# PEER gates: both buffers on their way to memory kept through the early down stage, their stores awaited at the first reload; one more modulation row in the search

## The chip, the cores and the metric

The kernel runs on one core of one Trainium2 chip. The metric is the device time of one execution in microseconds (us). In the text the engines are TensorE (PE, with PEld for its weight loads), VectorE (DVE), ScalarE (ACT), GpSimd (POOL) and SyncE (SP). VectorE, ScalarE and TensorE each work through their own instructions in order; they meet at semaphores.

## What is computed

The program computes three transformer blocks on 256 tokens of width 1024, one after the other. The change lies in the PEER feed-forward layer of the first block, which picks 16 of 128 x 128 experts for each of 8 heads and each token:

```python
q = (xt @ w_q).reshape(n_tok, PEER_HEADS, 2, PEER_KEY_HALF)
s = jnp.einsum('thpk,pnk->thpn', q, sub_keys)
top_s, top_i = lax.top_k(s, PEER_TOPK)
...
best_s, best_pos = lax.top_k(cand_s, PEER_TOPK)
experts = jnp.take_along_axis(cand_i, best_pos, axis=-1)
gates = jax.nn.softmax(best_s, axis=-1)
...
hid = gelu(einsum('chkd,cd->chk', u_tab[ec], xc))
y = einsum('chk,chkd->cd', gc * hid, v_tab[ec])
```

and in the modulation vectors of the third block, `mod = silu(c) @ ada_w[layer] + ada_b[layer]`, which need nothing but inputs and so are computed early, in 24 rows of 512 columns, wherever an engine has room.

## The kernel before, in words

The kernel does not gather experts. It computes the hidden value of every expert column group for all tokens and multiplies it by a dense table of gates that is zero where an expert was not picked. The 128 x 128 experts are worked as 128 groups ("keys" in the code, experts below) of 128. The first 40 (`EARLY`) have their hidden values (`early_up`, then GELU into `acted` or `late`) computed ahead, beside the search and the spread of the gates.

Weights come through one ring of four chunks of 2 MB (`ring`), filled by SyncE in the order of one stream. A chunk is asked for when the chunk four places ahead of it is released, which happens at the first matmul of the chunk behind that one, so SyncE is three chunks ahead of TensorE. The stream's order in these stages is written out by hand: `SEARCH_CHUNKS` for the search and `SPREAD_CHUNKS` for the spread of the gates, where `u` is a chunk with the up weights of four early experts and `a` one modulation row (`ada_row`, 8 matmuls into bank 4, L1430).

Four stages matter here.

1. **The search** (L1569 on). VectorE finds the top 16 in two halves of tokens. TensorE meanwhile works through `SEARCH_CHUNKS`, and ScalarE takes each early expert through GELU (L1638). ScalarE works in order: 14 early experts, the exponential of the first half's scores (`found`, L1640), 14 more, the exponential of the second half. VectorE needs that exponential for the sum of gates (L1626). At the end TensorE transposes `found` (L1664) and ScalarE copies it to `expert`.
2. **The spread** (`spread_gates`, L1725). In 32 batches of eight tokens VectorE makes one-hot rows and columns, TensorE multiplies them into the dense gates (L1837), in 64 steps of four tokens, and ScalarE copies them out of PSUM: 16 of the 128 experts stay in `gates` (L1808), the other 112 go to one of two buffers, `away_first` and `away_last` (L1812), by turns of 16 tokens, and from there to `kept_gates` in memory (L1815). Behind the matmuls of every second step TensorE has a piece of `SPREAD_CHUNKS`: half an early expert or one modulation row. At its end ScalarE copies the ten rows summed so far into `mod` (L1820) and waits until the stores of `away_first` have landed (L1821), since that buffer lives in this stage only. TensorE ends with 18 warm-up matmuls (`keep_warm`, L558, products of ones that nobody reads).
3. **The early down stage** (`early_down`, L1865). For each of the 40 early experts VectorE scales its hidden values by the gates into `full` (L1918); ScalarE rounds `full` and the down weights to `hidden_hi` and `down_hi` (L1903, L1891), VectorE makes the remainders `down_lo` and `hidden_lo` (L1924, L1926), and TensorE adds three products to banks 4 to 7 (L1943, L1949, L1953). ScalarE splits the weights of the first expert and then waits for the stores of both buffers (L1899, L1900) ahead of the loop. Behind every eighth expert it reloads eight experts' gates from `kept_gates` (`load`, L1893), for use from expert 16 on.
4. **The feed-forward loop** (`feed_forward`, L1123) does the other 88 experts, with the rest of the rows on VectorE.

A stage is a block: all engines meet at its end before the next one starts.

Of the kernel before, what the change touches and what calls it, by code (L numbers as in the profile page):

```python
# [20 lines left out]
BF16 = mybir.dt.bfloat16  # L21
# [5 lines left out]
P = 128  # L27
TOKENS = 256
# [22 lines left out]
SPAN = 16  # L51
GROUP = 8
EARLY = 40
SEARCH_CHUNKS = "uuauuuauu"
SPREAD_CHUNKS = "auaauaauaaa"
FORWARD_CHUNKS = "ff" + 14 * "afff"
ROWS_ON_PE = (SEARCH_CHUNKS + SPREAD_CHUNKS).count("a")
LATE_ROWS = [n for n, kind in enumerate(FORWARD_CHUNKS) if kind == "a"]
# [336 lines left out]
def build(nc, d, widths, offsets):  # L395
    ctx = ExitStack()
    with ctx:
        names = {}

        def buffer(name, shape, dt=F32):  # L400

            names[name] = names.get(name, 0) + 1
            return nc.sbuf_tensor(name if names[name] == 1 else f"{name}_{names[name]}", shape, dt)

        def sbuf(name, shape, dt=F32, mem=ctx):
            return mem.enter_context(buffer(name, shape, dt))
# [1009 lines left out]
        def peer(mem):  # L1416
# [251 lines left out]
            with ExitStack() as dense:  # L1668
                gates = sbuf("gates", [P, KEPT // GROUP, TOKENS // SPAN, GROUP, SPAN], mem=dense)
                work = hT[:, 0:4, :].rearrange("p (a b) n -> p a b n", a=2)  # L1670
                with ExitStack() as early:
                    away_last = sbuf("away_last", [P, KEYS - KEPT, SPAN], mem=early)
                    late = sbuf("acted_late", [P, EARLY - n_early, TOKENS], mem=early)
                    acted_of = lambda e: acted[:, e, :] if e < n_early else late[:, e - n_early, :]
                    spread_gates(expert, key_no, gates, away_last, acted_of, ada_row, early_up)
                    early_down(acted_of, gates, work)
                buf_2, p = params("ln2", dense)
                row_sums = sbuf("row_sums", [P, 4, WIDE], mem=dense)
                feed_forward("peer", KEYS - EARLY, ACT.Gelu, x_parts, scale_by=gates, starts=False, work=work, ahead=(buf_2[:], d["ln2"]),
                             rows=(lambda k: cond_at[:, k, BAND - 1:BAND], one_at, row_sums))  # L1680
# [41 lines left out]
            act.dma_start(gates[:, slot].rearrange("p b j m -> p b (j m)"),  # L1722
                          src.rearrange("b p n -> p b n")).then_inc(gates_loaded[slot], 16)

        def spread_gates(expert, key_no, gates, away_last, acted_of, ada_row, early_up):  # L1725

# [16 lines left out]
            with signals("dve_step", "parts_ready", "columns_ready", "weighed", "placed", "placed_read", "early_ready", "early_read",  # L1745
# [3 lines left out]
                    buffer("number", [P, 2, TOKENS], BF16) as number, buffer("keys", [P, KEYS, near], BF16) as keys, \  # L1749
                    buffer("row_hot", [P, 2, batch // near, KEYS, near], BF16) as row_hot, \  # L1750
                    buffer("col_hot", [P, 2, batch // near, KEYS, near], BF16) as col_hot, \
                    buffer("col_gate", [P, 2, 3, batch // near, KEYS, near], BF16) as col_gate, \
                    buffer("away_first", [P, KEYS - KEPT, SPAN]) as away_first, nc.Block() as block:
                away = (away_first, away_last)
                gate_rest = away_last[:].rearrange("p j m -> p (j m)")[:, 0:2 * TOKENS].rearrange("p (a n) -> p a n", a=2)

                @block.sync
                def _(sp):
# [34 lines left out]
                @block.scalar  # L1793
                def _(act):
                    early = [n for n, (kind, _, half) in enumerate(extra) if kind == "u" and half % 2]

                    def keep_early(n):

                        if n in early:
                            e = early.index(n)  # L1800
                            act.wait_ge(early_ready, e + 1)
                            act.activation(acted_of(first_early + e), ps[:, 5 + e % 3, 0:TOKENS], ACT.Gelu).then_inc(early_read, 1)

                    for s in range(steps):
                        n, at = s // per_block, s % per_block * few
                        got = ps[:, s % 4, :].rearrange("p (m j) -> p j m", m=few)
                        act.wait_ge(placed, s + 1)
                        act.activation(gates[:, :, n, :, at:at + few], got[:, 0:KEPT, :].rearrange("p (g j) m -> p g j m", j=GROUP),  # L1808
                                       ACT.Copy)
                        if n >= 2 and at == 0:  # L1810
                            act.wait_ge(gates_stored[n % 2], 16 * (n // 2))
                        act.activation(away[n % 2][:, :, at:at + few], got[:, KEPT:KEYS, :], ACT.Copy).then_inc(placed_read, 1)  # L1812
                        if s % per_block == per_block - 1:
                            act.wait_ge(placed_read, s + 1)
                            act.dma_start(kept_gates[n], away[n % 2][:].rearrange("p j m -> p (j m)")).then_inc(gates_stored[n % 2], 16)  # L1815
                        if s % 2 and s >= 3:
                            keep_early(s // 2 - 1)
                    keep_early(batches - 1)
                    act.wait_ge(mod_ready, 1)
                    act.activation(mod[:], ps[:, 4, :], ACT.Copy)  # L1820
                    act.wait_ge(gates_stored[0], 16 * (blocks // 2))  # L1821

                @block.tensor
                def _(pe):
                    e = 0
                    row = first_row
                    keep_warm(pe, 23, 5)
                    for s in range(steps):
                        b = s // 2 % 2
                        if s % 2 == 0:  # L1830
                            pe.wait_ge(weighed, s // 2 + 1)
                        if s >= 4:
                            pe.wait_ge(placed_read, s - 3)
                        for m in range(few):
                            g, o = (s % 2 * few + m) // near, m % near
                            for a in range(3):
                                last = pe.matmul(ps[:, s % 4, m * KEYS:m * KEYS + KEYS], row_hot[:, b, g, :, o],  # L1837
                                                 col_gate[:, b, a, g, :, o], start=(a == 0), stop=(a == 2))
                        last.then_inc(placed, 1)
                        if s % 2 == 0 or s // 2 >= len(extra):  # L1840
                            continue
                        kind, _, half = extra[s // 2]
                        if half == 0:
                            w = stream.slot(stream.take(pe))
                        if kind == "a":
                            last = ada_row(pe, w, row)
                            row += 1
                            if row == ROWS_ON_PE:
                                last.then_inc(mod_ready, 1)
                        else:  # L1850
                            if half % 2 == 0 and e >= 3:
                                pe.wait_ge(early_read, e - 2)
                            last = early_up(pe, w, half // 2, range(4 * (half % 2), 4 * (half % 2) + 4), 5 + e % 3)
                            if half % 2:
                                last.then_inc(early_ready, 1)
                                e += 1
                        if half == 0:
                            stream.pending = True
                    pe.wait_ge(early_read, EARLY - first_early)
                    keep_warm(pe, 18, 5)  # L1860

        def early_down(acted_of, gates, work):

# [6 lines left out]
            with signals("full_ready", "high_ready", "hidden_ready", "down_done", "down_hi_ready", "down_split") as (  # L1870
# [12 lines left out]
                @block.scalar  # L1883
                def _(act):
                    def split_down(j):

                        if j % 4 == 0:
                            stream.wait(act, first + j // 4)
                        if j >= 2:
                            act.wait_ge(down_done, j - 1)  # L1890
                        act.activation(down_hi[:, j % 2, :], raw(j), ACT.Copy).then_inc(down_hi_ready, 1)  # L1891

                    def load(group):  # L1893

                        act.wait_ge(full_ready, GROUP * (group + 1))
                        load_gates(act, gates, group % (KEPT // GROUP), group)

                    split_down(0)
                    for n, stored in enumerate(gates_stored):  # L1899
                        act.wait_ge(stored, 16 * (TOKENS // SPAN // 2))  # L1900
                    for j in range(EARLY):
                        act.wait_ge(full_ready, j + 1)
                        act.activation(hidden_hi[:, j % 2, :], full[:, j % 2, :], ACT.Copy).then_inc(high_ready, 1)  # L1903
                        if j % GROUP == GROUP - 1:
                            load(j // GROUP)
                        if j + 1 < EARLY:
                            split_down(j + 1)
# [22 lines left out]

                @block.tensor
                def _(pe):
                    keep_warm(pe, 10, 0)
                    for j in range(EARLY):
                        hi, lo = down_hi[:, j % 2, :], down_lo[:, j % 2, :]
                        pe.wait_ge(down_split, j + 1)
# [1890 lines left out]
```

## Time and profile before

| | |
|---|---|
| median of 3 runs | 3170.78 us (3165.64 to 3172.79) |
| profiled execution | 3165.71 us |
| its span in the trace | 3164.0 us |
| its mean granted TensorE clock | 0.981 of full |
| TensorE busy | 3001.0 us (95%) |
| VectorE busy | 2312.5 us (73%) |
| ScalarE busy | 1570.1 us (50%) |
| DMA mean | 206 GB/s |

Times in the trace are us from the start of the span. The search lies at 375 to 485, the spread at 485 to 598, the early down stage at 598 to 725. A row of the timeline has the start, the time that the group of instructions took, the engine (PEld, ACTq and SPq are TensorE's weight loads and the queues that issue DMAs), the line in the kernel, the output and inputs, and the count. In square brackets stands how long the engine was idle before it, and what released it. A DMA issue's own time is that of issuing; how long the transfer took to land is in the DMA views.

### The profile page before, as it was taken

What the parts mean: (1) busy time and instruction counts of PE and PEld (TensorE: products, weight loads), DVE (VectorE), ACT (ScalarE), POOL (GpSimd) and SP (SyncE); (2) the same over time, 40 slices, a digit from 0 to 9 for tenths busy, and PEclk for the clock granted to TensorE, in tenths of its full rate; (3) what the DMA queues carried; (4) which work ended last, traced back from release to release, by engine and by line L of the source; (5) the groups of instructions that cost most, each with busy time, mean ns of one, the idle gap of its engine ahead of it and who ended that gap; (6) DMA issues with size and microseconds to landing.
All of it is one profiled execution on the core that took longest, in us unless ns stands there. A gap on an engine that the chain in (4) does not pass through costs nothing. (4 is left out here: it accounts for less than half of the span.)

```text
span 3164.0 us, 45210 instructions
## 1 busy us (share of the span) xinstructions
PE 3001.0 (95%) x17980; PEld 2532.8 (80%) x17980; DVE 2312.5 (73%) x3604; ACT 1570.1 (50%) x2500; POOL 96.5 (3%) x135
## 2 busy tenths in 40 slices
PE   8999999999999999979999899989998889999997
PEld 7897887678888887757877688768886679999997
DVE  6466599668888886387765677757656768888887
ACT  4443313444444444264443544644345368878875
POOL 0000000000000001200000000000001000000000
PEclk9999999999999999899998999999999889999999
DMA  7344456866777764314542254424542068989895
GB/s 297 146 180 166 150 199 238 317 216 253 283 262 273 285 253 182 134 54 149 190 156 104 107 186 160 160 80 160 184 181 100 1 246 325 341 332 332 324 340 196
DMA packets 81262, 652.05 MB, mean 206 GB/s; under 512 B 6168, under 2 KB 35352, under 8 KB 38704
## 3 DMA queue, kind: packets, MB, share of 16 engines
q1 hardware_dynamic: 49872, 620.05, 52.5%
q10 hardware_dynamic: 31200, 29.36, 2.9%
q8 instruction: 132, 2.16, 0.3%
q14 instruction: 58, 0.48, 0.0%
HBM read 633.66 MB, written 15.73 MB: 205 GB/s over the span
## 5 line engine op out<-in xcount | busy, mean ns | idle before, releaser
L1238 PE MATMUL ps<-x_both,up_hi 128*128 128x512 f32 x1568 | 559.2, 396 | 2.4 <-DVE up_lo L1338 2.1
L369 DVE TENSOR_TENSOR weight_lo<-ring,weight_hi 128x1024 fp32r<-128x1024 f32 x236 | 289.5, 1238 | 231.6 <-ACT weight_hi L362 231.0
L1242 PE MATMUL ps<-x_both,up_lo 128*128 128x256 f32 x1568 | 440.7, 281 | 0.0
L1238 PEld LDWEIGHTS ps<-x_both,up_hi 128*128 128x128 f32 x1568 | 294.4, 188 | 76.6 <-DVE up_lo L1338 3.4
L362 ACT ACTIVATE weight_hi<-ring 128x1024 fp32r<-128x1024 f32 x236 | 245.6, 1053 | 162.4 <-PE ps L542 95.2
L1242 PEld LDWEIGHTS ps<-x_both,up_lo 128*128 128x128 f32 x1568 | 295.8, 189 | 6.3
L3529 DVE TENSOR_TENSOR up_lo<-ring,up_hi 128x1024 fp32r<-128x1024 f32 x242 | 294.3, 1217 | 5.1 <-ACT up_hi L3648 5.1
L520 PE MATMUL ps<-x_both,weight_hi 128*128 128x256 f32 x1024 | 291.2, 284 | 3.4 <-DVE weight_lo L369 2.5
L521 PE MATMUL ps<-x_both,weight_hi 128*128 128x256 f32 x1024 | 288.6, 282 | 0.0
L522 PE MATMUL ps<-x_both,weight_lo 128*128 128x256 f32 x1024 | 288.4, 282 | 0.0
L3446 PE MATMUL ps<-up_hi,taken_hi 128*128 128x256 f32 x968 | 285.6, 295 | 2.1 <-DVE seat L3533 2.1
L1256 PE MATMUL ps<-down_hi,hidden_hi 128*128 128x512 f32 x696 | 274.2, 394 | 1.3 <-DVE hidden_lo L1370 1.3
L3448 PE MATMUL ps<-up_hi,taken_lo 128*128 128x256 f32 x968 | 274.2, 283 | 0.0
L3447 PE MATMUL ps<-up_lo,taken_hi 128*128 128x256 f32 x968 | 274.2, 283 | 0.0
L1260 PE MATMUL ps<-down_lo,hidden_hi 128*128 128x512 f32 x696 | 272.9, 392 | 0.0
L3648 ACT ACTIVATE up_hi<-ring 128x1024 fp32r<-128x1024 f32 x242 | 256.0, 1059 | 25.4 <-PE ps L3448 24.9
L1338 DVE TENSOR_TENSOR up_lo<-ring,up_hi 128x1024 fp32r<-128x1024 f32 (+1 forms) x174 | 235.5, 1354 | 17.2 <-ACT up_hi L1299 17.2
L1343 DVE TENSOR_TENSOR down_lo<-ring,down_hi 128x1024 fp32r<-128x1024 f32 x174 | 212.4, 1221 | 24.4 <-ACT down_hi L1305 23.7
L1305 ACT ACTIVATE down_hi<-ring 128x1024 fp32r<-128x1024 f32 x174 | 183.7, 1056 | 64.2 <-PE ps L1264 64.1
L1264 PE MATMUL ps<-down_hi,hidden_lo 128*128 128x512 f32 x696 | 214.4, 389 | 0.0
L1299 ACT ACTIVATE up_hi<-ring 128x1024 fp32r<-128x1024 f32 (+1 forms) x174 | 201.0, 1156 | 5.6 <-PEq L1874 4.8
L520 PEld LDWEIGHTS ps<-x_both,weight_hi 128*128 128x128 f32 x1024 | 195.2, 191 | 7.2 <-DVE weight_lo L369 3.8
(552 smaller groups left out, 6318.9 us busy)
## 6 DMA issues: line engine op xcount, KB each, us to landing
ring<-in_stream SPq DMA_DIRECT2D x180, 2048.0 KB, 7.7
ring<-in_experts SPq DMA_DIRECT2D x121, 1536.0 KB, 8.6
ring<-in_stream SPq DMA_DIRECT2D x22, 1536.0 KB, 6.3
gates<-kept_gates ACTq DMA_DIRECT2D x14, 1024.0 KB, 9.0
kept_gates<-away_first ACTq DMA_DIRECT2D x8, 896.0 KB, 5.2
kept_gates<-away_last ACTq DMA_DIRECT2D x8, 896.0 KB, 7.7
params_mix<-in_mix SPq DMA_DIRECT2D x1, 3072.0 KB, 22.7
ring<-in_stream SPq DMA_DIRECT2D x4, 512.0 KB, 7.6
```

The source lines that it names most:

```text
L369: dve.tensor_tensor(self.place(self.lo, b), self.raw(b), self.place(self.hi, b), ALU.subtract).then_inc(self.split, 1)
L520: first = pe.matmul(out, hi[:, k, :], x_parts[0][:, k, :], start=(k == 0), stop=False)
L521: second = pe.matmul(out, hi[:, k, :], x_parts[1][:, k, :], start=False, stop=False)
L522: last = pe.matmul(out, lo[:, k, :], x_parts[0][:, k, :], start=False, stop=(k == DK - 1))
L1238: last = pe.matmul(out, hi[:, o:o + P], x_both[:, k, :, :].rearrange("p a n -> p (a n)"), start=(k == 0), stop=(k == DK - 1), skip_group_c ...
L1242: last = pe.matmul(out[:, 0:TOKENS], lo[:, o:o + P], x_hi[:, k, :], start=False, stop=(k == DK - 1), skip_group_check=True)
L1256: last = pe.matmul(out, hidden_hi[:, j % 2, tokens], hi[:, o:o + WIDE], start=(starts and i is None and j == 0), stop=False, skip_group_ch ...
L1260: pe.matmul(out, hidden_hi[:, j % 2, tokens], lo[:, o:o + WIDE], start=False, stop=False, skip_group_check=True)
L3446: pe.matmul(to, taken_hi[:, s % 3, k, :], hi, start=(k == 0), stop=False, skip_group_check=True)
L3447: pe.matmul(to, taken_hi[:, s % 3, k, :], lo, start=False, stop=False, skip_group_check=True)
L3448: last = pe.matmul(to, taken_lo[:, s % 3, k, :], hi, start=False, stop=(k == DK - 1), skip_group_check=True)
L3529: dve.tensor_tensor(up_part(up_lo, g, half), raw_up(g, half), up_part(up_hi, g, half), ALU.subtract).then_inc(up_split, 1)
```

## The change

The edit does four things. It allocates both `away` buffers outside of the spread stage, so that they live until the early down stage is over. It takes the wait for `gates_stored[0]` out of the end of the spread, and moves the waits for both stores from ahead of the early down loop into `load`, ahead of the first reload of gates (group 0, behind expert 7). It moves one modulation row from the end of `SPREAD_CHUNKS` (11 chunks before, 10 after) to `SEARCH_CHUNKS` (9 before, 10 after): the second row of the search now comes behind 16 early experts and a third behind 24, where the second stood behind 20. And it cuts the warm-up matmuls from 18 to 9 at the end of the spread and from 10 to 7 at the start of the early down stage. The number of rows that TensorE does (ten) and of early experts (28 and 12) stays.

```diff
--- before.py
+++ after.py
@@ -51,8 +51,8 @@
 SPAN = 16
 GROUP = 8
 EARLY = 40
-SEARCH_CHUNKS = "uuauuuauu"
-SPREAD_CHUNKS = "auaauaauaaa"
+SEARCH_CHUNKS = "uuauuauuau"
+SPREAD_CHUNKS = "auaauaauaa"
 FORWARD_CHUNKS = "ff" + 14 * "afff"
 ROWS_ON_PE = (SEARCH_CHUNKS + SPREAD_CHUNKS).count("a")
 LATE_ROWS = [n for n, kind in enumerate(FORWARD_CHUNKS) if kind == "a"]
@@ -1669,10 +1669,10 @@
                 gates = sbuf("gates", [P, KEPT // GROUP, TOKENS // SPAN, GROUP, SPAN], mem=dense)
                 work = hT[:, 0:4, :].rearrange("p (a b) n -> p a b n", a=2)
                 with ExitStack() as early:
-                    away_last = sbuf("away_last", [P, KEYS - KEPT, SPAN], mem=early)
+                    away = [sbuf(n, [P, KEYS - KEPT, SPAN], mem=early) for n in ("away_first", "away_last")]
                     late = sbuf("acted_late", [P, EARLY - n_early, TOKENS], mem=early)
                     acted_of = lambda e: acted[:, e, :] if e < n_early else late[:, e - n_early, :]
-                    spread_gates(expert, key_no, gates, away_last, acted_of, ada_row, early_up)
+                    spread_gates(expert, key_no, gates, away, acted_of, ada_row, early_up)
                     early_down(acted_of, gates, work)
                 buf_2, p = params("ln2", dense)
                 row_sums = sbuf("row_sums", [P, 4, WIDE], mem=dense)
@@ -1722,7 +1722,7 @@
             act.dma_start(gates[:, slot].rearrange("p b j m -> p b (j m)"),
                           src.rearrange("b p n -> p b n")).then_inc(gates_loaded[slot], 16)
 
-        def spread_gates(expert, key_no, gates, away_last, acted_of, ada_row, early_up):
+        def spread_gates(expert, key_no, gates, away, acted_of, ada_row, early_up):
 
 
 
@@ -1749,10 +1749,8 @@
                     buffer("number", [P, 2, TOKENS], BF16) as number, buffer("keys", [P, KEYS, near], BF16) as keys, \
                     buffer("row_hot", [P, 2, batch // near, KEYS, near], BF16) as row_hot, \
                     buffer("col_hot", [P, 2, batch // near, KEYS, near], BF16) as col_hot, \
-                    buffer("col_gate", [P, 2, 3, batch // near, KEYS, near], BF16) as col_gate, \
-                    buffer("away_first", [P, KEYS - KEPT, SPAN]) as away_first, nc.Block() as block:
-                away = (away_first, away_last)
-                gate_rest = away_last[:].rearrange("p j m -> p (j m)")[:, 0:2 * TOKENS].rearrange("p (a n) -> p a n", a=2)
+                    buffer("col_gate", [P, 2, 3, batch // near, KEYS, near], BF16) as col_gate, nc.Block() as block:
+                gate_rest = away[1][:].rearrange("p j m -> p (j m)")[:, 0:2 * TOKENS].rearrange("p (a n) -> p a n", a=2)
 
                 @block.sync
                 def _(sp):
@@ -1818,7 +1816,6 @@
                     keep_early(batches - 1)
                     act.wait_ge(mod_ready, 1)
                     act.activation(mod[:], ps[:, 4, :], ACT.Copy)
-                    act.wait_ge(gates_stored[0], 16 * (blocks // 2))
 
                 @block.tensor
                 def _(pe):
@@ -1857,7 +1854,7 @@
                         if half == 0:
                             stream.pending = True
                     pe.wait_ge(early_read, EARLY - first_early)
-                    keep_warm(pe, 18, 5)
+                    keep_warm(pe, 9, 5)
 
         def early_down(acted_of, gates, work):
 
@@ -1893,11 +1890,12 @@
                     def load(group):
 
                         act.wait_ge(full_ready, GROUP * (group + 1))
+                        if group == 0:
+                            for stored in gates_stored:
+                                act.wait_ge(stored, 16 * (TOKENS // SPAN // 2))
                         load_gates(act, gates, group % (KEPT // GROUP), group)
 
                     split_down(0)
-                    for n, stored in enumerate(gates_stored):
-                        act.wait_ge(stored, 16 * (TOKENS // SPAN // 2))
                     for j in range(EARLY):
                         act.wait_ge(full_ready, j + 1)
                         act.activation(hidden_hi[:, j % 2, :], full[:, j % 2, :], ACT.Copy).then_inc(high_ready, 1)
@@ -1930,7 +1928,7 @@
 
                 @block.tensor
                 def _(pe):
-                    keep_warm(pe, 10, 0)
+                    keep_warm(pe, 7, 0)
                     for j in range(EARLY):
                         hi, lo = down_hi[:, j % 2, :], down_lo[:, j % 2, :]
                         pe.wait_ge(down_split, j + 1)
```

## Rows read from the trace of the kernel before

**Rows 1.** The page's busy times: us, share of the span, instructions.
```profile
PE 3001.0 (95%) x17980; PEld 2532.8 (80%) x17980; DVE 2312.5 (73%) x3604; ACT 1570.1 (50%) x2500; POOL 96.5 (3%) x135
```

**Rows 2.** Timeline from 586 to 612: start, us, engine, line, operation.
```profile
586.80 6.99 SPq L314 DMA_DIRECT2D ring<-in_stream  x3
...
592.39 1.92 PE L1430 MATMUL ps<-ring,cond_at 128*32 128x512 f32 x16
...
593.18 0.33 ACTq L1815 DMA_DIRECT2D kept_gates<-away_last  x1
...
594.24 4.06 PE L562 MATMUL ps<-ones 128*128 128x512 bf16 x18
594.38 0.60 ACT L1820 ACTIVATE mod<-ps 128x512 f32<-128x512 f32 x1 [1.23 <-PE ps L1430]
...
598.58 1.06 ACT L1891 ACTIVATE down_hi<-ring 128x1024 fp32r<-128x1024 f32 x1 [3.60 <-PEq L1753]
598.60 2.32 PE L562 MATMUL ps<-ones 128*128 128x512 bf16 x10 [0.30 <-PEq L1753]
...
599.67 1.23 DVE L1924 TENSOR_TENSOR down_lo<-ring,down_hi 128x1024 fp32r<-128x1024 f32 x1 [0.64 <-ACT down_hi L1891]
604.87 0.42 ACT L1903 ACTIVATE hidden_hi<-hT 128x256 fp32r<-128x256 f32 x1 [5.23 <-DMA kept_gates<-away_last]
...
605.31 0.43 DVE L1926 TENSOR_TENSOR hidden_lo<-hT,hidden_hi 128x256 fp32r<-128x256 f32 x1 [4.42 <-ACT hidden_hi L1903]
...
605.89 0.77 PE L1943 MATMUL ps<-down_hi,hidden_hi 128*128 128x512 f32 x1 [4.97 <-DVE hidden_lo L1926]
...
611.14 0.40 PE L1943 MATMUL ps<-down_hi,hidden_hi 128*128 128x512 f32 x1
```

**Rows 3.** Windows: stretch, us, busy of PE to POOL, clock, DMA share, GB/s.
```profile
606.00:611.00 5.00, 5.00 (x12) 3.94 (x13) 1.97 (x4) 0.53 (x2) 0.00 (x0) 0.50 0.94 341
```

**Rows 4.** DMA issues from 584 to 607: count, KB each, median us to landing.
```profile
ring<-in_stream SPq DMA_DIRECT2D x4, 2048.0 KB, 12.2
kept_gates<-away_first ACTq DMA_DIRECT2D x1, 896.0 KB, 4.5
kept_gates<-away_last ACTq DMA_DIRECT2D x1, 896.0 KB, 11.6
```

**Rows 5.** Timeline of ScalarE around the second row of the search (at 447.82).
```profile
447.92 0.38 ACT L1638 ACTIVATE acted<-ps 128x256 f32<-128x256 f32 x1 [3.07 <-PE ps L1439]
453.43 0.38 ACT L1638 ACTIVATE acted<-ps 128x256 f32<-128x256 f32 x1 [5.12 <-PE ps L1439]
```

**Rows 6.** Timeline of the end of the search.
```profile
477.60 0.38 ACT L1638 ACTIVATE acted<-ps 128x256 f32<-128x256 f32 x1 [3.07 <-PE ps L1439]
...
479.30 0.31 ACT L1640 ACTIVATE found<-found 128x128 f32<-128x128 f32 x1
479.74 2.29 DVE L1624 TENSOR_REDUCE found<-sums 128x128 f32<-128x2048 f32 x1
```

**Rows 7.** Timeline of TensorE after two other pauses.
```profile
725.61 1.89 PE L562 MATMUL ps<-ones 128*128 128x512 bf16 x8 [0.32 <-PEq L1874]
...
2450.87 12.33 PE L3256 MATMUL ps<-q_dec,k_dec 128*128 128x64 f32 x64 [4.77 <-DVE k_dec L3036]
```

**Rows 8.** Timeline of TensorE from the search into the spread, and VectorE's first batch.
```profile
477.40 0.49 PE L1664 MATMUL ps<-ident,found 128*128 128x128 f32 x3
...
482.96 0.90 PE L1664 MATMUL ps<-ident,found 128*128 128x128 f32 x3 [5.07 <-DVE found L1628]
...
485.13 6.67 PE L562 MATMUL ps<-ones 128*128 128x512 bf16 x23 [1.26 <-PEq L1570]
...
488.77 1.89 DVE L1790 TENSOR_TENSOR col_gate<-col_hot,gate_part 128x1024 bf16<-128x1024 bf16 x3
...
491.63 1.54 PE L1837 MATMUL ps<-col_gate,row_hot 128*128 128x128 bf16 x24
```

**Rows 9.** Windows: the same columns as in rows 3, in the spread.
```profile
520.00:560.00 40.00, 40.00 (x439) 31.32 (x438) 38.77 (x63) 17.30 (x55) 0.00 (x0) 1.00 0.81 318
```

## The prediction, made before the change was run

> **What bounds the kernel now.** I read the page's busy times first. TensorE is busy for 3001 of the 3164 us of the span and VectorE for 2312 [rows 1], so nearly everywhere a change is worth what it takes off TensorE's way, and elsewhere only what it takes off a pause of TensorE. The change touches the end of the spread stage (`spread_gates`) and the start of the stage after it (`early_down`), so I read the order of time there [rows 2]. TensorE places the last tokens, runs one modulation row for 1.92 us from 592.39, then 18 warm-up matmuls for 4.06 us from 594.24 to 598.30. The block ends, and `early_down` begins on ScalarE at 598.58. TensorE gives ten more warm-ups and then sits idle for 4.97 us, until 605.89. The reader should follow the releasers back: TensorE waits for `hidden_lo`, that for `hidden_hi` on ScalarE, and `hidden_hi` at 604.87 is released by the store of `away_last`, 5.23 us after ScalarE had been ready. That wait is lines 1899 and 1900, which stand ahead of the loop. Third, the granted clock [rows 3]: from 606 to 611 it is 0.50, the lower level, 1.2 GHz, after TensorE's pause. The first expert of the loop therefore takes from 605.89 to 611.14, 5.25 us. Fourth, the transfers [rows 4]: the store of `away_last`, issued at 593.18 [rows 2], needed 11.6 us, because three ring loads of 2 MB were issued within 586.80 to 593.79 and share the DMA with it; the last store of `away_first` needed 4.5 us and had landed at about 591.0. For the search stage I read how far TensorE's work is from the end of VectorE's [rows 5, 6].
>
> **Part 1: the shorter end of the spread stage.** The row moved out ran behind the last placed tokens, with nothing of TensorE's beside it: 594.24 - 592.39 = 1.85 us of TensorE's path. Warm-ups go from 18 to 9: 18 took 4.06 us, a lone one about 0.38, so one more costs (4.06 - 0.38) / 17 = 0.2165 us and nine take 8 x 0.2165 + 0.38 = 2.11. That removes 1.95 us. TensorE now ends at 592.39 + 2.11 = 594.50 instead of 598.30: **3.8 us** earlier. What is late next? ScalarE's last copy out of PSUM and its DMA issue end at 593.51 (593.18 and 0.33 of issue), and the copy of `mod` (0.60 us [rows 2]) needs no later row any more: it ends near 594.1, 0.4 us ahead of TensorE. SyncE has one ring load fewer to issue there. The wait for `gates_stored[0]` that is taken out costs nothing now (that store had landed at about 591.0), so its removal is worth 0. A block's end does not itself wait for transfers: the store of `away_last` was under way across the end at 598.3 [rows 2, 4].
>
> **Part 2: the store wait moved to the first reload.** From the block's end at 598.30, ScalarE splits the first weights at 598.58 (1.06), VectorE follows at 599.67 (1.23) and ends at 600.90 [rows 2]. `hidden_hi` then no longer waits for anything but its turn: it would run from 599.67 to 600.09 beside VectorE's work. `hidden_lo` takes 0.43 and TensorE begins 0.15 behind it, as at 605.89. So TensorE's first real matmul stands 600.90 + 0.40 + 0.15 = 601.45, that is 3.15 us behind the block's end instead of 7.59: **4.44 us** gone. Seven warm-ups instead of ten cost 0.65 us less and end before 596.4; they are hidden under this chain either way, worth 0. New start of the first expert: 594.50 + 3.15 = 597.65 against 605.89, 8.24 us in all. The wait itself comes back at expert 7, where it stands on ScalarE ahead of one DMA issue and of `split_down(8)`, for which VectorE and TensorE would wait. It is reached after seven experts of some 2.7 us, at about 617, and the store had landed by 604.9 even with one more load in the way. Its cost is that of two waits already satisfied; no row isolates one, so between 0 and 0.1 us, and I take 0, since 12 us of margin cover it.
>
> **Part 3: the clock.** The first expert took 5.25 us at 1.2 GHz [rows 2, 3], which is 2.6 us at 2.4 GHz. TensorE's pauses there become 0.3 us at the block's end and 597.65 - 594.8 - 1.7 = 1.15 us behind the seven warm-ups. The nearest row is the next change of stage, at 725.61, where a pause of 0.32 us was followed by eight warm-ups in 1.89 us, at the full rate [rows 7]. So I take the clock as kept: **2.6 us** gained; the ends are 0 and 2.6.
>
> **Part 4: one more row in the search.** TensorE works there without a pause until 477.9 [rows 8]. A row costs it the distance between two results with a row between, less the usual one: (453.43 - 447.92) - (3.07 + 0.38) = 5.51 - 3.45 = 2.06 us [rows 5]. The new row stands behind the 16th expert, so the first half's exponential (behind the 14th) does not move. The second half's does: it ends now at 479.61 and would end at 481.67; VectorE, busy with its own reduction, asks for it at 482.03 [rows 6]. The row fits, with 0.36 us to spare: cost **0**, and if that cover were short at most 2.06. Its chunk is asked for three chunks ahead, over 20 us of TensorE's work, against 12.2 us for a load in the busiest stretch [rows 4]. Each later load keeps its moment in the spread stage and only moves up in what it carries, so that the last of the three loads of 586.80 to 593.79 disappears. The first chunk of `early_down` is asked for a whole group of experts earlier; the second at 586.80 and needed after four experts, near 608.
>
> TensorE's pause at 477.9 to 482.96 shrinks from 5.07 to 3.0 us. It is followed now by transposes of 0.90 us instead of 0.49 and by 23 warm-ups that take 6.67 us instead of 5.15 at the full rate, so that the first placement starts at 491.63 where its operands stood ready at 490.7 [rows 8]. The spread stage behind it leaves TensorE no gap (40.00 of 40 us busy, VectorE 38.77 [rows 9]), so a start earlier by up to 0.4 + 0.9 = 1.3 us would go through to the end. Whether 3 us keep the clock I can't tell: 4.77 us of pause at 2450.87 was followed by a long slow group, 12.33 us for 64 matmuls [rows 7]. Between a gain of 1.3 and a loss of 2 (the clock falling later, under the warm-ups) I take 0, as the pause was not shown to be short enough. The Trainium skill, "TensorE: Matmul & The Clock Gate", Part 1, says that the observation is free-running and does not start with the kernel's work, so equal pauses can end differently. By that sentence the sum would hold either end here; no run shown here tests it.
>
> **The sum.** 3.8 + 4.44 + 2.6 + 0 = 10.84 us off. What lies behind is ordered by TensorE's own progress and moves as a whole. The profiled execution took 3165.71 us (span 3164.0 and 1.7 around it), so it would be 3154.9. It stands 5.1 us below the median of the three runs shown, 3170.78; the median becomes **3159.9 us**, 0.34% less. The three runs lie 7.2 us apart, and about 0.2% (6.3 us) is what a measurement of this kernel can tell from no change.
>
> **The rivals.**
> A. The clock falls in spite of the warm-ups, because they are fewer: the first expert stays at 5.25 us. For it: a pause of TensorE came ahead of each slow stretch in these rows. Against it: the shortest pauses [rows 7]. The 2.6 us are lost: 3162.5.
> B. The added row isn't covered: the 0.36 us of margin are short, VectorE waits for its exponential and the whole rest slips by up to 2.06 us: 3162.0.
> C. The stall is moved, not removed: the store isn't down at expert 7, or the reload behind it is late for expert 16. `hidden` data of expert 8 then wait as they do now and most of the 4.44 us and the 2.6 us come back: 3167. Against it: 12 us of margin, and 2 MB less in the way.
> D. The edit doesn't do what it says, that is, some other wait holds the block's end or `hidden_hi`: then only the row and the warm-ups count, 3.8 us minus a longer pause behind them, 3167 to 3171. Against it: the profile names the store as the releaser.
> E. Slower: pauses all shift against the clock's changes. A slow stretch as at 2450.87 costs about 5 us (12 us at half the rate). From the third such new stretch on the gain is used up; with four and more, 20 - 10.8 = 9 us over: 3180. For it: slow stretches do follow pauses, and the search's and the spread's pauses change. Against it: the pauses here get shorter, and other stages keep theirs.
>
> **How the numbers follow.** Forecast 0.62; A 0.13; B 0.08; C 0.06; D 0.07; E 0.04. Forecast, A and B give 0.83, but the last two lie only 2 us inside the 6.3 us bound and the runs scatter by several us, so faster 0.80, within 0.2% 0.16, slower 0.04. The range reaches from 3159.9 less the 1.3 us of part 4 and half of the scatter (3.6 us), 3155, with a little more for a row or copy that I counted too high, 3153, up to rivals A and B with the same scatter, 3166.5.
>
> **What would show it.** TensorE's last warm-up of the spread stage ends near 594.5, `hidden_hi` of the first expert starts behind `down_hi` with no DMA named, TensorE's pause ahead of the first expert is near 1.2 us instead of 4.97, the granted clock there is 1.00 and the second expert starts near 600.3 instead of 611.14. In the search, `found` is exponentiated until 481.7 and VectorE names no wait for it in the second half. The prediction is wrong if `gate_sum` waits for `found` there, if a releaser `kept_gates` appears at expert 7, or if the clock is at 0.50 behind 597.

## The result and the profile after

The changed kernel takes 3158.78 us (median of 7 runs, 3156.89 to 3159.56), the kernel before 3169.24 us (7 runs, 3165.64 to 3172.79): 10.5 us less, ratio 0.9967 with a 95% interval of 0.9957 to 0.9977. The two profiled executions are 3165.71 and 3158.78 us, only 6.9 apart: the profiled execution of before lies at the fast end of its runs, whose lowest is 3165.64.

The place of the change, as the profile after has it, is this. The timeline's columns are as in [rows 2]; the last line of the first fence is the second expert of the loop.

```profile
586.19 3.67 SPq L314 DMA_DIRECT2D ring<-in_stream  x2
...
590.30 1.55 PE L1834 MATMUL ps<-col_gate,row_hot 128*128 128x128 bf16 x24
...
591.69 2.10 PE L562 MATMUL ps<-ones 128*128 128x512 bf16 x9
...
592.58 0.33 ACTq L1813 DMA_DIRECT2D kept_gates<-away_last  x1
592.95 0.60 ACT L1818 ACTIVATE mod<-ps 128x512 f32<-128x512 f32 x1 [0.40 <-ACT away_last L1810]
594.07 1.06 ACT L1888 ACTIVATE down_hi<-ring 128x1024 fp32r<-128x1024 f32 x1 [0.52 <-PEq L1752]
...
594.09 1.67 PE L562 MATMUL ps<-ones 128*128 128x512 bf16 x7 [0.30 <-PEq L1752]
595.03 0.40 ACT L1901 ACTIVATE hidden_hi<-hT 128x256 fp32r<-128x256 f32 x1
...
596.87 0.47 PE L1941 MATMUL ps<-down_hi,hidden_hi 128*128 128x512 f32 x1 [1.10 <-DVE hidden_lo L1924]
...
599.67 0.39 PE L1941 MATMUL ps<-down_hi,hidden_hi 128*128 128x512 f32 x1
```

Against [rows 2], `hidden_hi` no longer names a store, TensorE's pause ahead of the first expert is 1.10 us instead of 4.97, and that expert lasts from 596.87 to 599.67, 2.80 us instead of 5.25. The window below shows the clock, third from the end: 1.00 where [rows 3] had 0.50.

```profile
597.00:602.00 5.00, 5.00 (x23) 4.13 (x24) 2.90 (x5) 1.79 (x3) 0.00 (x0) 1.00 1.01 423
```

The moved wait stands where the first reload of gates is issued. The timeline there shows ScalarE going on without a pause of its own:

```profile
614.35 1.06 ACT L1888 ACTIVATE down_hi<-ring 128x1024 fp32r<-128x1024 f32 x1 [1.36 <-PE ps L1951]
614.74 0.39 ACTq L1722 DMA_DIRECT2D gates<-kept_gates  x1
615.32 0.40 ACT L1901 ACTIVATE hidden_hi<-hT 128x256 fp32r<-128x256 f32 x1
```

The store, issued at 592.58, took 11.6 us here too and landed at 604.2, 10.5 us ahead of that reload:

```profile
kept_gates<-away_last ACTq DMA_DIRECT2D x1, 896.0 KB, 11.6
```

And the end of the search, which now has one row more:

```profile
479.26 0.49 PE L1664 MATMUL ps<-ident,found 128*128 128x128 f32 x3
482.75 0.55 PE L1664 MATMUL ps<-ident,found 128*128 128x128 f32 x3 [3.00 <-DVE found L1628]
484.57 6.81 PE L562 MATMUL ps<-ones 128*128 128x512 bf16 x23 [1.27 <-PEq L1570]
491.21 1.54 PE L1834 MATMUL ps<-col_gate,row_hot 128*128 128x128 bf16 x24
...
481.16 0.31 ACT L1640 ACTIVATE found<-found 128x128 f32<-128x128 f32 x1
...
481.85 0.29 DVE L1626 TENSOR_REDUCE gate_sum<-found 128x8 f32<-128x128 f32 x1
```

`gate_sum` follows VectorE's own reduction with no wait named, as in [rows 6]; the exponential ends 0.35 us ahead of the time at which it is asked for.

To compare the two profiles without what happened earlier, I count from the first placement (491.63 in [rows 8], 491.21 here) to the second expert (611.14 in [rows 2], 599.67 here): 119.51 and 108.46 us, 11.05 less. At the first matmul of the feed-forward loop the changed kernel is 11.1 us ahead in time from the span's start (727.96 against 716.84).

### The profile page after: what moved, and what is told of

Its sections match the earlier page's. It is cut to its first block and busy times, and to the rows that moved or that the text cites. A ratio compares the mean times of both kernels' runs of the same rounds, so it can differ in the third digit from the quotient of the medians.

```text
span 3157.0 us, 45185 instructions
## 1 busy us (share of the span) xinstructions
PE 3003.0 (95%) x17968; PEld 2533.3 (80%) x17968; DVE 2313.1 (73%) x3604; ACT 1569.8 (50%) x2500; POOL 96.7 (3%) x135
```

## The experiments

All are timed against the kernel before, in two groups of four. The kernel before took 3167.96 us beside the first four and 3169.58 beside the last four.

**The wait alone.** Buffers and waits as in the change, rows and warm-ups as before. The cut is against the changed kernel:

```diff
-SEARCH_CHUNKS = "uuauuauuau"
-SPREAD_CHUNKS = "auaauaauaa"
+SEARCH_CHUNKS = "uuauuuauu"
+SPREAD_CHUNKS = "auaauaauaaa"
...
-                    keep_warm(pe, 9, 5)
+                    keep_warm(pe, 18, 5)
...
-                    keep_warm(pe, 7, 0)
+                    keep_warm(pe, 10, 0)
```

> The kernel before with both buffers living on and the store waits moved to the first reload; the row stays at the end of the spread and the warm-ups stay 18 and 10. Theory 1 (the parts add as in the prediction: a chain of 3.15 us behind the block's end, then the store wait, then the clock): the block ends as before near 598.3, the first expert starts near 601.5 instead of 605.9 and runs at the full clock, so 4.4 + 2.6 = 7.0 us faster. Rival (the store was late only because of the third ring load, and whoever removes that load gets the same): no different here, 7.0, but then row_only shows the same gain. Rival (the clock falls all the same): 4.4.

Measured: 3162.06 us against 3167.96, 5.9 us less, ratio 0.9985 (0.9976 to 0.9994). Timeline of that run:

```profile
597.23 2.32 PE L562 MATMUL ps<-ones 128*128 128x512 bf16 x10 [0.30 <-PEq L1752]
...
600.00 0.47 PE L1941 MATMUL ps<-down_hi,hidden_hi 128*128 128x512 f32 x1 [0.46 <-DVE hidden_lo L1924]
...
602.84 0.39 PE L1941 MATMUL ps<-down_hi,hidden_hi 128*128 128x512 f32 x1
```

The block ends at 596.93 and the first expert starts 3.07 us behind it, as in the changed kernel, where it was 7.59 in the kernel before. The second expert starts at 602.84, so the first takes 2.84 us, and the falling clock, the rival, is not there. Theory 1 holds in the trace: from the first placement (490.25) to the second expert it is 112.59 us against 119.51 in the kernel before, 6.92 less, where 7.0 were expected. The median shows 5.9; its interval allows 1.9 to 7.6 us.

**The row alone.** The kernel before with only this:

```diff
-SEARCH_CHUNKS = "uuauuuauu"
-SPREAD_CHUNKS = "auaauaauaaa"
+SEARCH_CHUNKS = "uuauuauuau"
+SPREAD_CHUNKS = "auaauaauaa"
```

> The kernel before with only the row moved from the spread to the search. Theory 1 (the store sets the first expert whatever TensorE does ahead of it): the store of away_last still lands near 604, as in the changed kernel, where it took 11.6 us too, so 0 to 1 us faster. Rival (the third ring load is what made the store late): it lands near 599 to 600, the pause of TensorE falls under 1.5 us and the clock is kept, 7 to 8 us faster.

Measured: 3167.91 us against 3167.96, ratio 1.0003 (0.9994 to 1.0012): no difference that the times can tell. Its timeline:

```profile
592.26 4.05 PE L562 MATMUL ps<-ones 128*128 128x512 bf16 x18
...
604.34 0.42 ACT L1903 ACTIVATE hidden_hi<-hT 128x256 fp32r<-128x256 f32 x1 [6.70 <-DMA kept_gates<-away_last]
...
605.36 0.76 PE L1943 MATMUL ps<-down_hi,hidden_hi 128*128 128x512 f32 x1 [6.44 <-DVE hidden_lo L1926]
```

And its DMA view for the store (count, KB, us to landing):

```profile
kept_gates<-away_last ACTq DMA_DIRECT2D x1, 896.0 KB, 11.1
```

The block ends 2.0 us sooner (596.31) and TensorE waits 1.5 us longer. The store is issued at 593.15 and takes 11.1 us, 0.5 less than before, although one 2 MB load is missing. That load had been issued at 593.45, 0.3 us behind the store. What the store shares the DMA with here are the two loads issued from 586.76 to 590.43: from 586 to 604 the DMA moves 6.05 MB, which is those two loads and the last two stores. The windows of this run show it at work until the store lands and no longer (the last two columns are the DMA's busy share and GB/s):

```profile
597.00:602.00 5.00, 1.92 (x9) 0.68 (x7) 1.25 (x2) 0.64 (x1) 0.00 (x0) 0.91 0.99 413
602.00:603.00 1.00, 0.00 (x0) 0.00 (x0) 0.00 (x0) 0.00 (x0) 0.00 (x0) 0.50 0.76 314
603.00:604.00 1.00, 0.00 (x0) 0.00 (x0) 0.00 (x0) 0.00 (x0) 0.00 (x0) 0.50 0.09 36
```

So the rival, that the third load made the store late, has fallen.

**The warm-ups alone.** The kernel before with 9 and 7 warm-ups in place of 18 and 10.

> The kernel before with only the warm-ups cut to 9 and 7. Theory 1: they stand ahead of the store wait, which still ends near 604.9; TensorE's pause grows from 5.0 to some 7.6 us, nothing gained: 0 (within 1 us), and the clock is at 0.50 for the first expert. Rival (warm-ups are on the path by themselves): 1.95 us faster.

Measured: 3167.43 us against 3167.96, ratio 0.9999 (0.9990 to 1.0008). The timeline shows the same wait for the store ahead of `hidden_hi` (6.46 us) and something else:

```profile
597.08 1.06 ACT L1891 ACTIVATE down_hi<-ring 128x1024 fp32r<-128x1024 f32 x1 [2.53 <-DMA ring<-in_stream]
...
605.62 0.77 PE L1943 MATMUL ps<-down_hi,hidden_hi 128*128 128x512 f32 x1 [7.71 <-DVE hidden_lo L1926]
```

The block ends at 595.94 now and ScalarE could begin at 596.2, but the first chunk of down weights has not landed before 597.1. With the row still in the spread, that chunk would have been the next wait, 0.9 us long, if the store's were gone. Moving the row asks for the chunk one group of experts sooner, and the wait is absent in the changed kernel.

**All but the moved wait.** The changed kernel with the store waits back ahead of the loop:

```diff
-                        if group == 0:
-                            for stored in gates_stored:
-                                act.wait_ge(stored, 16 * (TOKENS // SPAN // 2))
...
                     split_down(0)
+                    for n, stored in enumerate(gates_stored):
+                        act.wait_ge(stored, 16 * (TOKENS // SPAN // 2))
```

> The changed kernel with one part undone: the waits for both stores stand ahead of the early down loop again (the buffers live on). Theory 1: TensorE is ready at 596.9 but the first expert waits for the store until about 604, and the clock falls: 10 us slower than the changed kernel, 0 to 1 us faster than before. Rival (the ring load made the store late): the store lands near 599 to 600, 3 us slower than the changed kernel at the kept clock, 7 to 8 us faster than before.

Measured: 3168.63 us against 3167.96, ratio 1.0004 (0.9995 to 1.0013). `hidden_hi` waits 8.40 us for the store, TensorE 8.79, and the first matmuls are at the low rate:

```profile
603.68 0.42 ACT L1900 ACTIVATE hidden_hi<-hT 128x256 fp32r<-128x256 f32 x1 [8.40 <-DMA kept_gates<-away_last]
...
604.71 0.77 PE L1940 MATMUL ps<-down_hi,hidden_hi 128*128 128x512 f32 x1 [8.79 <-DVE hidden_lo L1923]
```

Counted from the first placement (491.33), the block ends 4.1 us sooner than in the kernel before, but the first expert starts only 0.9 sooner (113.38 us instead of 114.26), 0.7 of it because the store took 10.9 us here instead of 11.6. The rest is waited away. Gains by the medians: the wait alone 5.9 us, the row alone 0, the warm-ups alone 0.5 and row with warm-ups -0.7 (both inside their intervals around nothing); all together 10.5. The trace agrees for the wait (6.92 us) and for all together (11.05). The row and the warm-ups are worth their 4 us only once the store is out of the way.

**The changed kernel again,** as the measure for the next three, which ran beside it.

> The changed kernel as it is, a second time, as the measure for the other three of this call. Theory 1: about 0.33% under before again, the first expert near 597 at the full clock; what differs between two profiles of it is where the slow clock stretches of later stages fall, a few us of the span. Rival (the measured gain was partly chance): under 0.2%.

Measured: 3158.02 us against 3169.58, ratio 0.9960 (0.9947 to 0.9974). First expert from 596.53 at the full rate, first matmul of the feed-forward loop at 716.25, as in its first profile but for 0.6 us.

**No warm-ups** at the end of the spread and the start of the early down stage (both `keep_warm` lines taken out of the changed kernel).

> The changed kernel without any warm-ups at the end of the spread and the start of the early down stage. Theory 1 (they are there for the clock only): the block ends 0.2 us sooner, set by ScalarE's copy of mod; TensorE pauses for some 4.9 us ahead of the first expert, the clock falls to 0.50 and that expert takes 5.2 instead of 2.8 us: 2.4 us slower than the changed kernel. Rival (a pause of 4.9 us doesn't always cost the clock): 0.2 us faster, first expert at the full clock.

Measured: 3159.28 us against 3158.02 for the changed kernel, ratios to before 0.9966 (0.9954 to 0.9978) and 0.9960 (0.9947 to 0.9974), so the times alone don't tell the two apart. The trace does, first the timeline, then the window of the clock (third from the end):

```profile
597.26 0.77 PE L1939 MATMUL ps<-down_hi,hidden_hi 128*128 128x512 f32 x1 [4.76 <-DVE hidden_lo L1923]
...
602.45 0.40 PE L1939 MATMUL ps<-down_hi,hidden_hi 128*128 128x512 f32 x1
```

```profile
597.00:602.00 5.00, 4.74 (x13) 3.76 (x14) 2.25 (x5) 0.42 (x1) 0.00 (x0) 0.57 0.96 400
```

The pause of 4.76 us brings the clock down and the first expert takes 5.19 us instead of 2.80. Counted from the first placement (491.80, against 490.87 beside it) the first matmul of the feed-forward loop comes 226.96 - 225.38 = 1.6 us later, against 2.4 expected: 2.4 lost on the first expert, 0.2 gained on the block's end, 0.6 recovered in the experts behind. So the warm-ups pay by the clock, as far as this one pair of profiles shows.

**Two rows moved.** The changed kernel with one row more in the search:

```diff
-SEARCH_CHUNKS = "uuauuauuau"
-SPREAD_CHUNKS = "auaauaauaa"
+SEARCH_CHUNKS = "uuauuauuaau"
+SPREAD_CHUNKS = "auaauaaua"
```

> The changed kernel with one more row moved from the spread (its batch 30) to the search, ahead of the last four early experts. Theory 1 (0.35 us of cover is left in the search, each row costs 2.06 there): VectorE's gate_sum waits 1.7 us for found in the second half, the spread starts 1.7 us later and its end comes 1.6 to 1.8 us sooner for the missing row, as TensorE runs behind VectorE there: 0 in sum, within 0.5 us. Rival (the search has more cover than the row of the profile shows): no wait, 1.7 us faster. Rival (spread is set by VectorE, so the row there was free): 1.7 us slower.

Measured: 3157.80 us against 3158.02, ratio to before 0.9965 (0.9951 to 0.9978). The cover in the search is used up, and the wait that the prediction named as its sign is there:

```profile
482.22 0.28 DVE L1626 TENSOR_REDUCE gate_sum<-found 128x8 f32<-128x128 f32 x1 [1.46 <-ACT found L1640]
...
492.52 1.54 PE L1834 MATMUL ps<-col_gate,row_hot 128*128 128x128 bf16 x24
```

The first placement is 1.65 us later than in the changed kernel beside it (492.52 against 490.87). But this profile had begun the search 0.71 us sooner (TensorE's first matmul of the search at 375.24 against 375.95), and the distance stays 0.71 up to the added row. So the second row costs 2.36 us in the search: the wait of 1.46, and 0.93 at the lower clock behind it (the second transposes take 0.90 us instead of 0.55, the 23 warm-ups 7.39 instead of 6.81), less 0.03 elsewhere. From the first placement to the block's end it is 100.84 us (593.36) against 102.58 (593.45), 1.74 less. In sum the second row loses 0.6 us in the trace, a little over the 0.5 that Theory 1 allowed; the medians, 0.2 us apart, don't show it. The rival with more cover and the rival with a free row in the spread both fall. This run also has only one 2 MB load issued ahead of the store, at 587.69, and the store lands sooner:

```profile
kept_gates<-away_last ACTq DMA_DIRECT2D x1, 896.0 KB, 8.7
```

**The exponentials sooner.** The changed kernel with another order on ScalarE in the search:

```diff
-                        for t in range(TT):
-                            for e in range(t * n_early // TT, (t + 1) * n_early // TT):
-                                act.wait_ge(early_ready, e + 1)
-                                act.activation(acted[:, e, :], ps[:, 5 + e % 3, 0:TOKENS], ACT.Gelu).then_inc(early_read, 1)
-                            act.wait_ge(top_ready, t + 1)
-                            act.activation(found[:, t, 2, :], found[:, t, 2, :], ACT.Exp).then_inc(exped, 1)
+                        for e in range(n_early):
+                            act.wait_ge(early_ready, e + 1)
+                            act.activation(acted[:, e, :], ps[:, 5 + e % 3, 0:TOKENS], ACT.Gelu).then_inc(early_read, 1)
+                            if e + 1 in (12, 25):
+                                t = (12, 25).index(e + 1)
+                                act.wait_ge(top_ready, t + 1)
+                                act.activation(found[:, t, 2, :], found[:, t, 2, :], ACT.Exp).then_inc(exped, 1)
```

> The changed kernel with ScalarE's two exponentials of the search moved ahead: the first behind 12 early experts instead of 14, the second behind 25 instead of 28. Theory 1 (VectorE's 4.1 us wait for the first exponential is ScalarE's order and nothing else, and TensorE's early experts end 3.6 us ahead of VectorE): that wait goes, VectorE ends the search near 478.6, the transposes follow TensorE's last early expert without a pause, the block ends 3.0 us sooner, the clock stays at 1.00 and the 23 warm-ups behind take 5.2 instead of 6.8 us, so the first placement starts about 4.0 us sooner: 4.0 us faster than the changed kernel. Rival (the search is set by TensorE's early work alone): 0.4 us.

Measured: 3153.12 us (3152.00 to 3157.32) against 3158.02 for the changed kernel, ratio to before 0.9950 (0.9937 to 0.9964). That is 4.9 us between the medians, though the two intervals overlap. The timeline has the mechanism whole:

```profile
477.78 0.49 PE L1665 MATMUL ps<-ident,found 128*128 128x128 f32 x3
...
478.90 0.55 PE L1665 MATMUL ps<-ident,found 128*128 128x128 f32 x3 [0.63 <-DVE found L1628]
...
480.71 5.12 PE L562 MATMUL ps<-ones 128*128 128x512 bf16 x23 [1.27 <-PEq L1570]
486.31 1.55 PE L1835 MATMUL ps<-col_gate,row_hot 128*128 128x128 bf16 x24 [0.47 <-DVE col_gate L1789]
```

TensorE pauses 0.63 us instead of 3.02 between the transposes, the clock is kept, the 23 warm-ups take 5.12 instead of 6.81 us, and the first placement is at 486.31 instead of 490.87; at the feed-forward loop the lead is 716.25 - 711.71 = 4.5 us. Of this, 1.1 us is not the edit's: this profile began the search at 374.83, the one beside it at 375.95. What remains is 3.4 us, 2.4 for the wait and 1.0 for the clock behind it. VectorE names no wait for `found` any more. In the first half that wait was 4.1 us in the profiles before and after, but 2.4 in the changed kernel's second profile, where TensorE did its first eight early experts in 27.89 us instead of 29.58, at the full clock from the start. The 4.0 us expected were worked out for the wait of 4.1; in this pair it is 3.4, and the medians say 4.9. By its median this is the fastest of the kernels here.

## Why the prediction was right, and where its terms were off

- **The end of the spread** was forecast 3.8 us shorter. From the first placement to the block's end it is 106.67 us before (598.30 - 491.63) and 102.58 after (593.79 - 491.21): 4.09. Of the 0.3 us more, 0.2 lie in the spread itself and 0.1 in the join: the warm-ups begin 591.69 - 590.30 = 1.39 us behind the start of the last placement group, where 1.48 was assumed.
- **The store wait** was forecast at 4.44 us: block's end to first expert is 3.08 us instead of 7.59, 4.51. The run with the wait alone has 3.07, and the one with all but the moved wait shows no gain in its time.
- **The clock** was forecast at 2.6 us: 5.25 - 2.80 = 2.45. The run without warm-ups shows it lost with them gone (rival A in a harder form).
- **The row in the search** was forecast at 0 with 0.36 us to spare; 0.35 was left. The run with a second row shows that a row behind this cover costs 1.46 us of wait and 0.9 us of clock, so the margin was real and rival B had been near.
- **The first pause** was left between a gain of 1.3 and a loss of 2 us, and 0 was taken; that it came out near 0 is luck, as the forecast said it could not tell. The pause shrank to 3.00 us as worked out; the transposes took 0.55 instead of 0.90 us, but the clock fell behind them, and the 23 warm-ups took 6.81 instead of 6.67. In sum about 0.2 us gained. The run with the exponentials sooner shows the gain that was open here: its pause is 0.63 us and its warm-ups take 5.12.
- **The sum** of 10.84 us stands against 11.05 in the trace from the first placement to the second expert, and 10.5 between the medians. From there to the feed-forward loop 0.35 us go back (117.17 us instead of 116.82); no row says where.
- **Rival C** (the stall is moved) had 12 us of margin; it was 10.5. **Rival D** fell with the run of the wait alone. **Rival E** did not come in the medians. It shows between single profiles: from the feed-forward loop's first matmul to the end it is 2436.0 us before, 2440.2 and 2440.5 in the two profiles of the changed kernel, and 2435.7 to 2443.1 over the ten profiles of this study, whose code behind that point is the same. Counted in windows of 2 us, the lower clock takes 98 to 126 us of that rest, and more of it goes with a longer rest (105 us before, 122 after; correlation 0.83), but that this is the cause is only argued. Because of this spread the two profiled spans differ by 7.0 us and not by 11.
- **One step was wrong** without harming the sum: the prediction said that three ring loads held the store up, and that one load fewer eases it. The store took 11.6 us after as before, 11.1 with the row alone and 10.9 with row and fewer warm-ups. What counted were the loads issued ahead of it: with two rows moved only one stands there, and the store took 8.7 us. Had the forecast relied on the row to shorten the wait, as the rival in the run of the row alone did, it would have been 7 to 8 us off.

## What to carry to other kernels

When a stall ends last, everything that is cut ahead of it is worth nothing until the stall is gone: cost the edits in the order in which their waits end, not one by one, and test each alone. Let a buffer live on and put the wait for its store where its data are first needed again; the price is room in SBUF, and the check is that the landing time lies well ahead of the new place. A pause of TensorE is worth more than its own length where the clock falls with it, so a few warm-ups across a change of stage can pay (1.6 us here), but only if they aren't what ends last. And before two profiles are compared, look for the instruction from which they run alike: here single profiles of the same code stood up to 1.7 us apart by the clock at the start of the search.

## What the runs showed of the hardware

- A store of 896 KB took 4.5 to 5.1 us with no 2 MB load issued in the 20 us ahead of it and one issued 0.3 us behind it, 8.7 us behind one such load issued 4.5 us earlier, and 10.9 to 11.8 us behind two issued 3 and 6 us earlier. With a third load 0.3 us behind it the last figure is 11.6 to 11.8, without it 10.9 to 11.6.
- The same pause can end differently. In the search TensorE stood still for 3.00 us in the changed kernel and 3.02 us in the one without warm-ups, which is the same code up to there. In the first the transposes behind it took 0.55 us at the full rate and the clock fell later; in the second it had fallen within the pause (0.90 us). With two rows moved the pause was shorter, 2.73 us, and the transposes took 0.90 us all the same. The windows (clock third from the end), of the changed kernel first:

```profile
482.00:485.00 3.00, 0.98 (x5) 0.55 (x6) 1.06 (x5) 0.94 (x3) 0.00 (x0) 0.94 0.00 0
```

```profile
482.00:485.00 3.00, 0.90 (x3) 0.50 (x3) 0.77 (x3) 0.94 (x3) 0.00 (x0) 0.50 0.00 0
```

The Trainium skill, "TensorE: Matmul & The Clock Gate", Part 1, says that the observation is free-running and doesn't start anew with the kernel. Equal pauses with unequal ends agree with that; no run here shows the observation itself.
